# First two projections of a 512-token network by blocks of input and weights, with the first norm, the third weight chunk and the recurrence constant moved

## The reference, cut to what matters

```python
h = rms_norm(x, norm_g[layer])
p = h @ w_in[layer]
c_q, c_kv, k_r, gate_a, dil_qkv, gate_b = jnp.split(p, split_points, axis=-1)
```

```python
log_a = -LRU_C * r * jax.nn.softplus(-lam.astype(jnp.float32))
```

## Time and profile before

| | us |
|---|---|
| median of 3 runs | 2188.02 |
| lowest and highest of them | 2185.24, 2188.34 |
| the profiled execution | 2189.06 |
| its span, first to last instruction | 2187.3 |
| TensorE busy | 2118.7 (97%) |
| TensorE weight loads busy | 1749.1 (80%) |
| VectorE busy | 1160.8 (53%) |
| ScalarE busy | 779.8 (36%) |
| GpSimd busy | 65.9 (3%) |

### The profile page before, as it was taken

One profiled execution on the slowest core, in us unless ns is written; L12 is line 12 of the kernel. 1 busy time (PEld: TensorE's weight loads), 2 busy tenths in 40 slices (PEclk: granted clock), 3 DMA queues, 4 the chain that ended last, 5 costly groups with the idle time before them and its releaser, 6 DMA issues.

```text
span 2187.3 us, 28242 instructions
## 1 busy us (share of the span) xinstructions
PE 2118.7 (97%) x11681; PEld 1749.1 (80%) x11681; DVE 1160.8 (53%) x1565; ACT 779.8 (36%) x1243; POOL 65.9 (3%) x92
## 2 busy tenths in 40 slices
PE   6999999999999999999999998999999998999998
PEld 5888878678888888688888887788688887888887
DVE  4654557655555557655444445776743446333333
ACT  3251343543152424643222224353633244222222
POOL 0101000000101000000000003000000002000000
PEclk9999999999999999999999999999999999999999
DMA  4423212112413122022333224234022222232321
GB/s 149 117 69 100 78 58 74 42 43 77 135 40 116 59 77 80 24 65 87 96 96 97 96 99 141 77 116 135 21 77 97 96 96 78 86 98 95 101 99 69
DMA packets 156466, 189.03 MB, mean 86 GB/s; under 512 B 4099, under 2 KB 145733, under 8 KB 156229
## 3 DMA queue, kind: packets, MB, share of 16 engines
q1 hardware_dynamic: 151296, 174.34, 25.2%
q0 software_dynamic: 4608, 13.00, 2.0%
q10 hardware_dynamic: 452, 0.15, 0.0%
HBM read 182.20 MB, written 7.36 MB: 87 GB/s over the span
## 4 chain that ended last, share of the span: by engine, by line
PE 87%; DVE 6%; ACT 3%; issue 2%; POOL 1%; DMA 1%; POOLq 0%; SPq 0%; DVEq 0%; ACTq 0%
PE PS L898 25%; PE PS L900 24%; PE PS L899 24%; PE PS L1010 4%; PE PS L1051 2%; PE PS L1022 2%; POOL X L866 1%; PE PS L906 1%; PE PS L910 1%; PE PS L907 1%; DVE WL L1828 1%; PE PS L1162 1%; ACT PR L1438 1%; DMA ARENA<-in_x 1%; ACT PR L1435 0%
## 5 line engine op out<-in xcount | busy, mean ns | idle before, releaser
L898 PE MATMUL PS<-UH,WH 128*128 128x512 f32 x1616 | 635.2, 393 | 6.2 <-DVE WL L1828 5.1
L900 PE MATMUL PS<-UH,WL 128*128 128x512 f32 x1616 | 630.1, 390 | 0.0
L899 PE MATMUL PS<-UL,WH 128*128 128x512 f32 x1616 | 629.5, 390 | 0.0
L1365 ACT ACTIVATE WH<-WS 128x2048 fp32r<-128x2048 f32 x103 | 197.3, 1916 | 621.8 <-PE PS L900 603.2
L898 PEld LDWEIGHTS PS<-UH,WH 128*128 128x128 f32 x1616 | 303.9, 188 | 72.4 <-issue 8.7
L1828 DVE TENSOR_TENSOR WL<-WS,WH 128x2048 fp32r<-128x2048 f32 x103 | 235.8, 2289 | 228.7 <-ACT WH L1365 228.5
L900 PEld LDWEIGHTS PS<-UH,WL 128*128 128x128 f32 x1616 | 303.7, 188 | 63.7
L899 PEld LDWEIGHTS PS<-UL,WH 128*128 128x128 f32 x1616 | 303.9, 188 | 62.4 <-issue 0.7
L2093 DVE TENSOR_TENSOR WL<-WS,WH 128x2048 fp32r<-128x2048 f32 x44 | 100.7, 2288 | 149.8 <-ACT WH L1521 149.8
L1521 ACT ACTIVATE WH<-WS 128x2048 fp32r<-128x2048 f32 x44 | 84.4, 1917 | 248.9 <-PE PS L900 246.7
L898 PE MATMUL PS<-WH,UH 128*128 128x256 f32 x416 | 118.5, 285 | 0.0
(11 more groups left out here) (304 smaller groups left out, 3071.0 us busy)
## 6 DMA issues: line engine op xcount, KB each, us to landing
WS<-in_ffn_w SPq DMA_DIRECT2D x66, 1024.0 KB, 5.2
WS<-in_w_in SPq DMA_DIRECT2D x64, 1024.0 KB, 5.3
WS<-in_w_out SPq DMA_DIRECT2D x8, 1024.0 KB, 5.1
WS<-in_w_gate SPq DMA_DIRECT2D x8, 1024.0 KB, 5.4
WS<-in_w_attn_out SPq DMA_DIRECT2D x4, 1024.0 KB, 5.2
WS<-in_w_lru_out SPq DMA_DIRECT2D x4, 1024.0 KB, 5.4
WS<-in_w_o SPq DMA_DIRECT2D x4, 1024.0 KB, 5.1
bias_skewed<-bias_rows POOLq DMA_DIRECT2D x1, 3072.0 KB, 15.0
```

The source lines that it names most:

```text
L898: nc.tensor.matmul(dst, sh, mh, start=start, stop=False, skip_group_check=True)
L899: nc.tensor.matmul(dst, sh, ml, start=False, stop=False, skip_group_check=True)
L900: return nc.tensor.matmul(dst, sl, mh, start=False, stop=stop, skip_group_check=True)
L1365: nc.scalar.activation(WH[:, c % 2, 0:kt * n], WS[:, c % 2, 0:kt * n], ACT.Copy).then_inc(w_hi, 1)
```

## The change

- x is loaded in four blocks of 256 features; behind each, the matching quarter (two steps k) of chunks 0 and 1. All this, then chunk 2 and the constant vectors, in SyncE's queue; ScalarE keeps the identity and the first gains. GpSimd's rotation table and mask wait for the last block of x.
- Chunk 2 has a place of its own, `THIRD`, in what is later the attention's result, and chunk 3 takes slot 1.
- TensorE turns blocks 0 and 1, runs eight products whose result nobody reads, and takes the first two products in turn, two steps k of (q,0) and two of (k,0), with blocks 2 and 3 turned in between. The norm's sum stands behind the last step of (q,0), the constant vectors and bias row behind it, the norm's spread between the last two steps of (k,0).
- ScalarE, not VectorE, copies the turned input to `X`, and per block makes the high parts, both quarters of weights and the squares; VectorE per block the low parts and the sums of squares. The turned blocks lie in pairs 2 and 3.
- VectorE's `vectors` and `bias_rows` stand behind the norm's `inverse` and chunk 2's low part; chunk 3's high part follows the norm's copy on ScalarE, and its low part stands ahead of the rotations.
- `softplus` and its exponential stand behind the first attention's `merge`.

```diff
@@ make_plan
-        pl.unit(("xt", k), "d")
+        pl.aside(("xt", k), "a", 2 + k % 2)
@@ places
+        THIRD = view(9216, 2048)
+        def landing(c):
+            return 16 * (c // 2)
+        def staged(c, columns):
+            return THIRD[:, 0:columns] if c == 2 else WS[:, c % 2, 0:columns]
+        def first_part(t, c, f):
+            return slot(t, c, KD, CW)[:, 2 * f:2 * f + 2, :]
@@ block.sync
-            for r in range(NT):
-                sp.dma_start(XIN[:, r, :], a["x"][0].rearrange("(i r) d -> r i d", r=NT)[r]).then_inc(x_in, 16)
+            for f in range(4):
+                feats = slice(f * CW, (f + 1) * CW)
+                sp.dma_start(XIN[:, :, feats], a["x"][0][:, feats].rearrange("(i r) d -> i r d", r=NT)
+                             ).then_inc(x_in[f], 16)
+                for c in range(2):
+                    sp.dma_start(slot(WS, c, KD, CW)[:, 2 * f:2 * f + 2, :],
+                                 chunk_source(pl.chunks[c][0])[:, 2 * f:2 * f + 2, :]).then_inc(first_in[f], 16)
+
+            sp.dma_start(THIRD.rearrange("p (k n) -> p k n", k=KD), chunk_source(pl.chunks[2][0])).then_inc(landed[0], 16)
...
+                    sp.dma_start(ROWS[r:r + m, at_row // P, :], src[done:done + m, :]).then_inc(consts_in, 16)
...
-            c = 0
+            c = 3
@@ block.gpsimd
+            pool.wait_ge(x_in[3], 16)
             pool.dma_start(TAB, a["rotation"]).then_inc(tabs_in, 16)
@@ block.tensor
+            def idle_products(n):
+                for _ in range(n):
+                    nc.tensor.matmul(bank(3)[:, 0:P], IDN[:, :], ONES[:, :], start=True, stop=True, skip_group_check=True)
+            def input_turned(f):
+                key = ("xt", f)
+                pe.wait_ge(x_in[f], 16)
+                if f == 1:
+                    pe.wait_ge(small_dve, 1)
+                if f >= 2:
+                    pe.wait_ge(act_out, pl.act_out["xt", f - 2])
...
+            def first_step(c, k):
+                key = pl.chunks[c][0]
+                pe.wait_ge(lo_done, pl.lo[("x", 0), k])
+                if k < 6:
+                    pe.wait_ge(first_lo, k // 2 * 2 + c + 1)
+                else:
+                    weights(c)
+                for m in range(2):
...
+            def vectors_turned():
+                pe.wait_ge(act_out, pl.act_out["xt", 3])
+                pe.wait_ge(consts_in, 16 * vector_dmas)
...
+            input_turned(0)
+            input_turned(1)
+            idle_products(8)
+            for k in range(0, KD, 2):
+                for c in range(2):
+                    first_step(c, k)
+                    if c == 1 and k == 6:
+                        norm_spread(("x", 0))
+                    first_step(c, k + 1)
+                    if c == 0 and k < 4:
+                        input_turned(2 + k // 2)
+                    if c == 0 and k == 6:
+                        norm_sum(("x", 0), KD)
+                        vectors_turned()
@@ block.scalar
+            table(ACT.Copy)
...
+                    for f in range(4):
+                        ready(("xt", f))
+                        took(("xt", f), nc.scalar.activation(X[:, 2 * f:2 * f + 2, :], pair(("xt", f)), ACT.Copy))
+                        for k in (2 * f, 2 * f + 1):
+                            hi_of_gained(("x", L), k, (act_out, pl.act_out["xt", f]))
+                        act.wait_ge(first_in[f], 32)
+                        for c in range(2):
+                            nc.scalar.activation(first_part(WH, c, f), first_part(WS, c, f), ACT.Copy
+                                                 ).then_inc(first_hi if f < 3 else w_hi, 1)
+                        squares(("x", L), lambda k: X[:, k, :], (2 * f, 2 * f + 1))
...
+                table(ACT.Sqrt)
...
                 hi_of_chunk(c0 + 2)
                 rms(("x", L), D)
                 copy_inverse(("x", L))
+                if L == 0:
+                    hi_of_chunk(c0 + 3)
@@ block.vector
+                            tt(first_part(WL, c, f), first_part(WS, c, f), first_part(WH, c, f).bitcast(F32),
+                               ALU.subtract).then_inc(first_lo if f < 3 else w_split, 1)
+                        add_squares(("x", L), 2 * f, 2 * f + 2)
...
+                inverse(("x", L))
+                lo_of_chunk(c0 + 2)
                 if L == 0:
                     vectors()
                     bias_rows()
-                inverse(("x", L))
-                lo_of_chunk(c0 + 2)
...
+                if L == 0:
+                    lo_of_chunk(c0 + 3)
...
-                        if L == 0 and hh == 0 and i == 1:
-                            softplus()
...
                     merge(L, hh)
+                    if L == 0 and hh == 0:
+                        softplus()
```

More of the change, by code:

```diff
@@ L500, in pair @@
             return bank(2 * pl.pair[key], 2).rearrange("p (a b) -> p a b", a=2)
-        x_in = sem("x_in")
+        x_in = [sem(f"x_in{f}") for f in range(4)]
+        first_in = [sem(f"first_in{f}") for f in range(4)]
+        first_hi = sem("first_hi")
+        first_lo = sem("first_lo")
         identity_in = sem("identity_in")
@@ L1175, in _ @@
                         last = nc.tensor.transpose(pair(key)[:, m, r * P:(r + 1) * P],
-                                                   XIN[:, r, (2 * j + m) * P:(2 * j + m + 1) * P], IDN[:, :])
+                                                   XIN[:, r, (2 * f + m) * P:(2 * f + m + 1) * P], IDN[:, :])
                 last.then_inc(acc_ready, 1)
+            def first_step(c, k):
[6 more added lines that the diff above has]
+                for m in range(2):
+                    part = slice(m * P, (m + 1) * P)
+                    last = three(pair(key)[:, m, :], slot(WH, c, KD, CW)[:, k, part], slot(WL, c, KD, CW)[:, k, part],
+                                 UH[:, k, :], UL[:, k, :], k == 0, k == KD - 1)
+                if k == KD - 1:
+                    last.then_inc(acc_ready, 1)
+            def vectors_turned():
+                pe.wait_ge(act_out, pl.act_out["xt", 3])
+                pe.wait_ge(consts_in, 16 * vector_dmas)
+                for i in range(2):
+                    n = min(P, NVEC - i * P)
+                    last = nc.tensor.transpose(bank(5)[:, i * P:i * P + n], ROWS[0:n, i, :], IDN[0:n, 0:n])
+                last.then_inc(small_pe, 1)
+                pe.wait_ge(rel_in, 48)
+                nc.tensor.matmul(bank(6)[0:QH, 0:384], TBL, ONEHOT, start=True, stop=True).then_inc(small_pe, 1)
+            input_turned(0)
[12 more added lines that the diff above has]
+                        vectors_turned()
             pe.wait_ge(const_ok, 2)
@@ L1205, in _ @@
                                           norm=("x", L) if hh == 0 and i == 1 else None)
[L1206 to L1211, removed]
-                            last.then_inc(small_pe, 1)
-                            pe.wait_ge(rel_in, 48)
-                            nc.tensor.matmul(bank(7)[0:QH, 0:384], TBL, ONEHOT, start=True, stop=True
-                                             ).then_inc(small_pe, 1)
                     pe.wait_ge(rope_done, pl.rope["k", L, hh, 2])
@@ L1350, in hi_of_chunk @@
                 _, kt, n, _ = pl.chunks[c]
-                act.wait_ge(landed[c % 2], 16 * (c // 2 + 1))
-                if c >= 2:
-                    act.wait_ge(acc_ready, pl.acc[pl.chunks[c - 2][3]])
+                act.wait_ge(landed[c % 2], landing(c))
+                act.wait_ge(acc_ready, pl.acc[pl.chunks[c - 2][3]])
                 if pl.chunks[c][0][0] == "ukv":
@@ L1518, in hi_in_loop @@
                     c = c0 + b
-                    act.wait_ge(landed[c % 2], 16 * i + 16 * ((c + 2) // 2 + 1))
+                    act.wait_ge(landed[c % 2], 16 * i + landing(c + 2))
                     act.wait_ge(acc_ready, 2 * i + (pl.acc[f, "w1", 0] + b))
```

103 lines of the change are left out of this document (50 added, 53 removed).

## The result

| | before | after |
|---|---|---|
| median (lowest, highest), run side by side | 2188.18 (2185.24, 2188.36) | 2174.81 (2173.72, 2176.38) |
| ratio, 95% interval | | 0.9939 (0.9928 to 0.9951) |
| the profiled execution | 2189.06 | 2176.38 |
| its span | 2187.3 | 2174.6 |
| TensorE busy | 2118.7 | 2118.1 (97%) |

The change is faster by 13.4 us. The last two rows are the account to keep: of the 12.7 us by which the spans differ, 66.71 - 54.95 = 11.8 lie ahead of (q,1), and 0.9 behind it. The profiled execution of the changed kernel is the longest of its four.

What follows compares the result with a forecast made beforehand. TensorE's start bounds the kernel: serial input, low clock and a 1.38 us stall ahead of (q,1). 12.25 + 1.38 = 13.6 us off 2189.06 gives 2175.5; the median, 1.04 lower, 2174.4; range 2171.6 to 2178.0.

Steps and rivals of the forecast that it cites:

- The sum of 13.6: Total gain in us: 12.25 up to the start of (v,0), plus 1.38 for chunk 3's stall ahead of (q,1).
- the signs that the prediction named: What the changed profile should show in first product, x1's transposes, clock, waits at vectors, (v,0), (q,1) and the blocks.
- x1 lands between 7.3 and 8.8: At the start: input's second block arrives then, from 359 GB/s after the ramp and a possible slowdown by GpSimd's small pieces.
- third rival: Input stream slower, or constants land after 35; x1 at 11 costs about 2.7 us, giving 2177.1; chance 0.10.
- The gains: At the start: the first gains arrive at 5.7 (bounds 5.2 and 6.4), and are turned at 6.0.
- The idle products: On TensorE behind x1's transposes: eight f32 products of two passes, bounded by 1.8 us (fast) and 4.0 us (slow).
- bound of 14.4: Latest start of the first product on TensorE, in a range from 11.7 and not before 12.1; 13.3 was taken.
- clock cost of 0.4: At the first products: 0.4 us charged for low clock, bounds 0 and 2.7.
- Rivals 2 and 5: Clock low at the first products, 2176.8 to 2178.3, chance 0.13 (2); through both products, 2195, chance 0.02 (5).
- rival 4: First two products: ScalarE's chain per block takes over 6.4 us instead of 4.6, TensorE waits at each; 2184.4, chance 0.04.
- norm sum: On TensorE behind product 0: 0.4 us, half of the 0.8 for eight passes.
- The new stall at (v,0): (v,0) starts at 41.4, 1.8 us after TensorE is free, behind chunk 2's low part, vectors and bias row on VectorE.

Runs made afterwards that it cites:

- e9: The changed kernel unaltered, run again on the chip of the three combined versions: 2175.96, ratio 0.9948.
- e1: Changed kernel with GpSimd's transfer of the sinks issued behind the rotation table and mask: 2173.43, ratio 0.9931.
- e3: Changed kernel with the constants' copies and bias row ahead of the norm's inverse and chunk 2's low part on VectorE: 2175.85, ratio 0.9944.
- v3: Changed kernel with sinks late, constants ahead of the norm's inverse, the eight idle products out, three between x0's and x1's transposes: 2171.90, ratio 0.9930.
- e2: Changed kernel without the eight idle products: 2174.92, ratio 0.9941.
- e4: Changed kernel with chunk 3's high and low part back in their old places, the low part behind VectorE's two rotations: 2179.77, ratio 0.9961.
- e5: Changed kernel with the softplus and its exponential back in their old places, behind the rotations of (q,0) and (k,0): 2175.15, two runs, ratio 0.9938.
- e6: Changed kernel without a place of its own for chunk 2, which is loaded into slot 0: 2176.01, two runs, ratio 0.9942.
- e8: Kernel before the change, with 29 unread products between the input's transposes and the first product: 2184.07, ratio 0.9984.
- v2: Changed kernel with the sinks' transfer late and the constants and bias row ahead of the norm's inverse: 2174.54, ratio 0.9938.

## Why the prediction was right, and where it was not

**The time.** Forecast 2174.4, measured 2174.81, and the gain where it was put, ahead of (q,1). The stretch behind it didn't change by more than the scatter just shown. But in the profiled execution (q,1) starts at 54.95, not at 53.1, and 0.9 us later in e9 than forecast too. The sum of 13.6 was 1.8 too large by that trace and 0.9 by e9's (66.71 - 54.02 = 12.7). Two things outside the sum made most of it up: the part behind was 0.9 us shorter than before, and the profiled execution lies 1.57 above its median where the forecast took 1.04, another 0.5. What is left is the 0.4 between 2174.4 and 2174.81. The closeness to 0.4 is thus luck; that the gain lies ahead of (q,1) and comes from TensorE's idle time there is not. Of the signs that the prediction named, three were missed: x1's transposes at 7.3 to 8.8 (11.02), first product at 12 to 14.5 (16.26), (q,1) at 52 to 54 (54.95).

**The input: the step that failed.** "x1 lands between 7.3 and 8.8": measured 10.97, and 10.37 to 11.20 in the other traces with the sinks in their place. The working took 359 GB/s after the ramp, and saw that the rate falls to 152 GB/s in the same place of before "with the small pieces of GpSimd's first transfers in flight", but gave that only 1.5 us as an upper bound. What it did not do is ask what that dip costs the bytes behind it: e1 shows 2.5 us for 8 KB, and the pairs of traces 0.8 to 2.7. Only the third rival had x1 at 11, at a chance of 0.10, and it is this rival's mechanism that took place, in part: the price was 2.7 us per its own account, and x1 came 2.7 later than the 8.3 I took. The gains were wrong the other way, 4.4 instead of 5.7, which made block 0 ready 0.9 us early and, behind x1, gained nothing.

**The idle products.** I took a value between 1.8 and 4.0; they took 3.28 us in the changed kernel, 2.2 to 3.4 in the chains of the others that have all eight: at the low clock each takes 0.43, and where the sum is shortest (e3) it rises among the first of them. First product at 16.26, beyond the bound of 14.4; of the 3.0 over 13.3 x1 alone would be 2.7. In return the clock cost of 0.4 fell away: no product behind them is slow.

**The clock.** Right in kind. Read from the lengths of transposes and products, it rose 5.0 us after x1's first transpose in the changed kernel, and between 2.7 and 5.6 us after it in the other traces but v3, where idle products stand ahead of x1 and it rose about 1.9 after it; I had 4.4. The rule of the Trainium skill, TensorE: Matmul & The Clock Gate, Part 4 (PE-mode transpose), by which transposes don't count, is not borne out: before the change from 421 to 272 ns in the earlier trace rows nothing but transposes had run, from 13.76 on. In e2 full clock is there 3.5 us after x1's first transpose, with eight transposes and three products in between and an idle time of 3.3 us right before them. Rivals 2 and 5, 14 slow products at the start or the low clock throughout, did not occur in any trace of the changed kernel's variants; four slow products, in e2, are the most.

**The two products.** From the first product to the end of (k,0) 42.27 - 16.26 = 26.0 us; forecast 26.2, or 25.8 without the 0.4 for slow products. The blocks never wait, so rival 4 is out. Within this the norm sum was mis-sized: its eight passes, the same as in the kernel before, took 0.8 us (36.98 to 37.79) and not half of that; constants and bias row took 38.95 - 37.79 = 1.2 instead of 1.0. The constants' landing cost nothing, their wait at 35 was met.

**The new stall at (v,0).** Forecast 1.8 us, behind the bias row; measured 1.1, with that releaser, and e3 shows that it is the order on VectorE. Counted from the end of product 0, VectorE was as quick as worked out (6.4 us to the start of (v,0), forecast 6.6), while TensorE took 42.27 - 36.98 = 5.3 to the end of (k,0) instead of 4.7, for the norm sum and the constants; so the two differ by 1.1 and not by 1.9.

**Chunk 3, the softplus, the third place.** The stall of 1.38 is gone, and e4 shows it would have been 1.9. No cost of the softplus shows in either place (e5). The third place is free and needless (e6): the working had the chunk wanted at 35 without asking whether slot 0 was filled by then anyway.

**From before's side.** The gain of the start was told as one sum. The waits divide it: TensorE's listed waits up to (q,1) were 6.4 + 7.1 + 6.5 + 1.4 = 21.4 us before and are 4.4 + 4.4 + 0.9 = 9.7 in the changed kernel, 11.7 less, which is nearly the whole 11.8. The 3 us of low clock that e8 shows are gained on top, and the 3.3 us of idle products spend them again. No run takes back the blocks alone, so this largest term rests on the waits in the two traces and not on an experiment.

## What to carry to other kernels

When the start is cut into blocks and the second block's transposes stand ahead of the first product, the second block's arrival decides, not the first one's: look in the slices for a stretch where the DMA engines are busy and the rate is low, find the small transfer that is in flight there, and put it behind the data that TensorE waits for. Products that keep the clock up belong in a gap in which TensorE would idle, and not behind the last operation on which the first real product waits: here three in the gap cost nothing that shows, eight behind it cost 1.7 to 2.5 us net. Where the rest of the kernel scatters by more than the edit is worth, compare the start of the same product in two traces and the time behind it apart.

## What the runs showed of the hardware that I had not expected

- A transfer of 8 KB, the same 64 bytes to each of 128 partitions, took the input stream from 341 and 372 GB/s to 69 and 128 in two slices of 1 us, and delayed x1 from 8.50 to 10.97. The dip is in all seven traces with that transfer early and in none of the four with it late. With it gone from there, x1's landing still varied between 8.50, 8.97 and 9.62 among kernels whose transfers up to that point are the same.
- The clock's rise varies: 2.7 us (e3) to 5.6 us (v2) after x1's first transpose, in kernels with the same queue on TensorE up to there.
- The granted clock of the slices doesn't show the low level at the very start: it reads 1.00 from 4 to 17 us in the changed kernel, as it does in the earlier trace rows at 15, while transposes take 421 ns in one place and 272 in another. Between 26 and 32 of before it reads 0.50 and products take 0.43, so there the two agree. At the start I go by the lengths.
- In a kernel of 2175 us whose TensorE is busy for 97%, the clock still falls to its low level for a few us in the middle. Slices of 2 us between (q,1) and TensorE's last work add up to 14 to 24 us at the low level per trace: two stretches in all fourteen, a further one in ten, in one of two places. The time behind (q,1) goes with that one, 2118.0 to 2119.1 us without it and 2119.3 to 2120.8 with it.
- A filler that stops short: with 14 unread products that end 3.1 us before the next work, six of nine runs were as long as before (2188.15 to 2188.80); with 29, without the gap, the median was 2184.07. That the clock fell in the gap in those six is not traced.
